# A hybrid HGRN2/Hyena inference step on one core: the prompt's spectrum and the gating on GpSimd, one w_out tile between the inverse transforms, and two products by halves

## The chip, the cores and the metric

The kernel runs on one core of one Trainium2 chip. The metric is the device time of a whole execution in microseconds (us), median over the runs shown. Inside the core five engines run their own instruction streams and meet only at semaphores: TensorE (PE), VectorE (DVE), ScalarE (ACT), GpSimd (POOL) and SyncE (SP), the last of which only issues DMAs. PE writes its results to eight PSUM banks, DVE and ACT empty them.

## What is computed

One layer of a diffusion backbone for two groups of tokens, a prompt of 128 and a sample of 512, held together as 640 columns (five tiles of 128). Weights and activations are fp32. Cut to what matters here:

```
proj = h @ w_in                      # q, forget gates, values, gate, and hy (v, x1, x2)
o_hg = HGRN2 scan of both directions, normed, * silu(g)       # 512 channels
u    = x1 * v
z    = long_conv(u, kern) + hy_d * u # by FFT: transform, * spectrum of kern, transform back
y_hy = x2 * z * rsqrt(mean((x2 * z)**2) + eps) * hy_norm_w    # 512 channels
x    = x + g1 * (concat(o_hg, y_hy) @ w_out)
x    = x + g2 * convffn(rmsnorm(x) * (1 + sc2) + sh2)
```

## The kernel before, in words

Every engine's program is written out by hand, in order, inside one function `build`, with semaphore waits between them; nothing is scheduled by a planner. An fp32 product is made of three products of rounded halves (`w_hi`, `w_lo` and `h_hi`, `h_lo`): `split_product` issues them, `split_hi` (ACT) and `split_lo` (DVE) make the two halves of a weight unit of 128 x 1024, in four slots used in turn. `link` makes an engine wait for its own last instruction.

The stretch that the change touches lies between the HGRN2 heads and the second norm, from 386 to 475 us of the profiled execution. It does this:

- The product with `w_out` is cut into two halves of its input channels. The first half (`o_hg`) is made first: ten output tiles of 128 tokens x 512 columns (five token tiles times two column halves `n`), in PSUM banks 6 and 7 in turn. Each is copied by ACT into `x1` (`raw_taken`), multiplied with the gate row `grow1` on DVE (`gate_raw`), and a DMA of GpSimd's queue with an adding write then puts the residual `x` on top (`ld_res`).
- Meanwhile DVE multiplies the sample's spectrum `U` with the filter's (`multiply(0)`, `multiply(1)`, ten instructions each, the second of which raises `zspec_ready` to 2) and the prompt's spectrum `Up` with its own filter (seven instructions, `zspec_ready` 3).
- The inverse transforms follow on PE, one pair for each block `c` of 128 channels: `z_sample(c)` (8 matmuls, 16 records in the trace, for each of four blocks) and `z_prompt(c)`, in two pairs of banks. ACT takes them out (`zc`, which gives `z_taken` and `z_ready`), DVE makes `x2 * z` (`yhy_ready`) and splits it into `h_hi`, `h_lo` (`split_y`, `y_split`), ACT squares it into the one buffer `sq` (`ysq_ready`), and PE sums the squares over the channels with a column of ones (`sum_channels(c)`, `ysq_used`).
- `mix(i)` is the second half of the product with `w_out` for token tile `i`: both column halves, four channel blocks each. `mix_tile(i)` on DVE scales it, gates it, and adds it to `x1`; norm, transposes (`turn_tile`) and the first FFN products (`half_product`) follow.

Of the kernel before, what the change touches and what calls it, by code (L numbers as in the profile page):

```python
# [385 lines left out]
def build(nc, io):  # L386
# [12 lines left out]
    with ctx:  # L399
# [407 lines left out]
        def _(eng):  # L807
# [72 lines left out]
            eng.wait_ge(sem("zspec_ready"), 3)  # L880
# [10 lines left out]
        def _(eng):  # L891
# [60 lines left out]
            eng.wait_ge(sem("silu_in"), 1)  # L952
            A(gate_c, gate_c, ACT.Exp).then_inc(sem("silu_exp"), 1)
# [6 lines left out]
            eng.wait_ge(sem("bound_in"), 1)  # L960
            A(bound[:, 1, :], bound[:, 0, :], ACT.Exp).then_inc(sem("bound_exp"), 1)
# [155 lines left out]
            for n in range(2):  # L1117
                for i in range(NT):
                    eng.wait_ge(sem("hg_mixed"), n * NT + i + 1)
                    A(x1[:, n, i, :], ps[:, HG_BANKS[(n * NT + i) % 2], :], ACT.Copy).then_inc(sem("raw_taken"), 1)  # L1120
                for k in range(2):
                    split_hi(UNIT_WOUT + 4 + 2 * n + k)


# [238 lines left out]
        def _(eng):  # L1363
# [145 lines left out]
            eng.wait_ge(sem("bound_exp"), 1)  # L1509
# [188 lines left out]
            eng.wait_ge(sem("up_ready"), 1)  # L1698
            r, t = prod[:, 0, 0, :], prod[:, 1, 0, :]
            link(V.tensor_tensor(r, Up[:, 0, :], kspec_p[:, 0, :], ALU.mult))  # L1700
            link(V.tensor_tensor(t, Up[:, 1, :], kspec_p[:, 1, :], ALU.mult))
            link(V.tensor_tensor(r, r, t, ALU.subtract))
            link(V.tensor_tensor(t, Up[:, 0, :], kspec_p[:, 1, :], ALU.mult))
            link(V.tensor_tensor(Up[:, 1, :], Up[:, 1, :], kspec_p[:, 0, :], ALU.mult))
            link(V.tensor_tensor(Up[:, 1, :], Up[:, 1, :], t, ALU.add))
# [989 lines left out]
```

## Time and profile before

| | |
|---|---|
| median of 3 runs | 913.55 us (912.89 to 916.66) |
| the profiled execution | 912.88 us, of which the span of the trace is 911.1 us |
| PE busy | 887.6 us, 97% of the span |
| DVE busy | 717.0 us, 79% |
| ACT busy | 443.3 us, 49% |
| GpSimd busy | 38.9 us, 4%, 58 instructions |
| granted TensorE clock, mean | 0.996 of full speed |

The busy times of different engines overlap and can't be added. PE is busy for nearly all of the span, so what counts is where PE waits, and for whom. The times of day in the rows below are microseconds from the start of the span.

### The profile page before, as it was taken

How to read it: one execution, taken by the hardware profiler on the slowest of the kernel's cores; microseconds unless marked ns; L12 is line 12 of the kernel's file. 1: busy time of each engine (PE TensorE's matmuls, PEld its weight loads, DVE VectorE, ACT ScalarE, POOL GpSimd, SP SyncE). 2: the span in 40 equal slices, each digit the busy share in tenths (PEclk: the TensorE clock that was granted, in tenths of full speed). 3: DMA queues.
4: the chain of work that ended last, by engine and by line, in shares of the span. 5: the costliest groups of instructions: out<-in, count | busy, mean ns of one | idle time of the engine just before them, and what ended most of it. 6: DMA issues, size and time to landing. Idle time of an engine off the chain costs nothing.

```text
span 911.1 us, 14075 instructions
## 1 busy us (share of the span) xinstructions
PE 887.6 (97%) x5374; PEld 788.7 (87%) x5374; DVE 717.0 (79%) x911; ACT 443.3 (49%) x710; POOL 38.9 (4%) x58
## 2 busy tenths in 40 slices
PE   7999999999999999999899999999999999999997
PEld 4479898898898898688779999999999999998885
DVE  5744755966966985699678899999999999988645
ACT  5745324334343323332276756556565656565443
POOL 2200000100000000002000000000000000000000
PEclk9999999999999999999999999999999999999999
DMA  8765233144134244325511232233313232345703
GB/s 297 244 217 174 83 126 138 37 157 145 63 122 145 91 164 137 89 70 112 144 46 48 76 131 99 97 110 114 115 62 130 108 111 88 131 152 202 261 0 116
DMA packets 39275, 112.76 MB, mean 124 GB/s; under 512 B 4471, under 2 KB 12663, under 8 KB 38568
## 3 DMA queue, kind: packets, MB, share of 16 engines
q1 hardware_dynamic: 33944, 93.58, 30.3%
q0 software_dynamic: 4800, 17.99, 6.5%
q8 instruction: 43, 0.70, 0.3%
q10 hardware_dynamic: 464, 0.30, 0.1%
q14 instruction: 24, 0.20, 0.1%
HBM read 101.48 MB, written 10.37 MB: 123 GB/s over the span
## 4 chain that ended last, share of the span: by engine, by line
PE 84%; DVE 9%; ACT 3%; issue 2%; DMA 1%; ACTq 0%; DVEq 0%; POOLq 0%
PE ps L2005 19%; PE ps L2006 19%; PE ps L2007 19%; PE ps L2505 14%; PE ps L2226 4%; PE ps L2025 2%; PE ps L2086 2%; PE ps L2238 1%; PE ps L2363 1%; DMA part<-in_rates 1%; DVE w_lo L1377 1%; PE ps L2033 1%; PE ps L2246 1%; DMA w<-in_hy_w 1%; ACT xn L1154 1%
## 5 line engine op out<-in xcount | busy, mean ns | idle before, releaser
L2005 PE MATMUL ps<-h_hi,w_hi 128*128 128x320 f32 x620 | 196.3, 317 | 2.8 <-DVE w_lo L1377 1.4
L2007 PE MATMUL ps<-h_hi,w_lo 128*128 128x320 f32 x620 | 191.6, 309 | 0.0
L2006 PE MATMUL ps<-h_lo,w_hi 128*128 128x320 f32 x620 | 191.5, 309 | 0.0
L2005 PEld LDWEIGHTS ps<-h_hi,w_hi 128*128 128x128 f32 x620 | 116.6, 188 | 4.1 <-issue 3.1
L2006 PEld LDWEIGHTS ps<-h_lo,w_hi 128*128 128x128 f32 x620 | 116.6, 188 | 0.0
L2007 PEld LDWEIGHTS ps<-h_hi,w_lo 128*128 128x128 f32 x620 | 116.4, 188 | 0.0
L1868 DVE TENSOR_TENSOR w_lo<-raw,w_hi 128x1024 fp32r<-128x1024 f32 (+1 forms) x53 | 64.2, 1212 | 18.6 <-ACT w_hi L1220 17.6
L1220 ACT ACTIVATE w_hi<-raw 128x1024 fp32r<-128x1024 f32 (+1 forms) x53 | 55.5, 1047 | 31.8 <-PE ps L2007 31.7
L1377 DVE TENSOR_TENSOR w_lo<-raw,w_hi 128x1024 fp32r<-128x1024 f32 x44 | 53.4, 1224 | 6.4 <-ACT w_hi L904 5.2
L2005 PE MATMUL ps<-w_hi,h_hi 128*128 128x512 f32 x120 | 49.6, 413 | 2.0 <-DVE h_lo L1734 2.0
L904 ACT ACTIVATE w_hi<-raw 128x1024 fp32r<-128x1024 f32 x44 | 45.8, 1057 | 4.4 <-DMA raw<-in_slots 2.4
L2007 PE MATMUL ps<-w_hi,h_lo 128*128 128x512 f32 x120 | 47.4, 395 | 0.0
L2006 PE MATMUL ps<-w_lo,h_hi 128*128 128x512 f32 x120 | 47.3, 394 | 0.0
L1868 DVE TENSOR_TENSOR w_lo<-wsum,w_hi 128x1024 fp32r<-128x1024 f32 x38 | 46.4, 1221 | 1.0 <-ACT w_hi L1220 0.4
L2505 PE MATMUL ps<-t_hi,w_hi 128*128 128x320 f32 x152 | 47.0, 309 | 0.1
L2005 PE MATMUL ps<-t_hi,w_hi 128*128 128x320 f32 x152 | 47.0, 309 | 0.0
L2006 PE MATMUL ps<-t_lo,w_hi 128*128 128x320 f32 x152 | 47.0, 309 | 0.0
L2007 PE MATMUL ps<-t_hi,w_lo 128*128 128x320 f32 x152 | 47.0, 309 | 0.0
L2505 PE MATMUL ps<-h_hi,w_lo 128*128 128x320 f32 x152 | 47.0, 309 | 0.0
L2505 PE MATMUL ps<-t_hi,w_lo 128*128 128x320 f32 x152 | 47.0, 309 | 0.0
L2505 PE MATMUL ps<-t_lo,w_hi 128*128 128x320 f32 x152 | 47.0, 309 | 0.0
L2505 PE MATMUL ps<-h_lo,w_hi 128*128 128x320 f32 x152 | 46.9, 309 | 0.0
(320 smaller groups left out, 2067.2 us busy)
## 6 DMA issues: line engine op xcount, KB each, us to landing
raw<-in_slots SPq DMA_DIRECT2D x138, 512.0 KB, 4.7
acts<-actf POOLq DMA_DIRECT2D x22, 320.0 KB, 2.5
raw<-in_slots SPq DMA_DIRECT2D x24, 256.0 KB, 6.5
xf<-acts SPq DMA_DIRECT2D x12, 320.0 KB, 6.6
wsum<-acts SPq DMA_DIRECT2D x10, 320.0 KB, 7.7
xin<-in_x_sample SPq DMA_DIRECT2D x4, 512.0 KB, 11.2
grow<-gates POOLq DMA_DIRECT2D x2, 1024.0 KB, 12.3
x<-in_x_sample POOLq DMA_DIRECT2D x2, 1024.0 KB, 13.7
```

The lines of the kernel that those rows point to most:

```text
L904: A(w_hi[:, n % SPLITS, :], src, ACT.Copy).then_inc(sem("hi_ready"), 1)
L1154: A(xn[:, i % 2, :].rearrange("p (n c) -> p n c", c=HW), x1[:, :, i, :], ACT.Copy, scale=stat[:, 1, 1, i:i + 1]).then_inc(sem("xn_ready"), 1)
L1220: A(split_target(w_hi, t, slot), src, ACT.Copy).then_inc(sem("hi_ready"), 1)
L1377: V.tensor_tensor(w_lo[:, n % SPLITS, :], raw[:, r % RING, :], w_hi[:, n % SPLITS, :].bitcast(F32), ALU.subtract).then_inc(sem("lo_ready"), 1)
L1868: link(V.tensor_tensor(split_target(w_lo, t, slot), src, split_target(w_hi, t, slot).bitcast(F32), ALU.subtract), "lo_ready")
L2005: mm(out, lhs[0], rhs[0], start=first, stop=False)
L2006: mm(out, lhs[0], rhs[1], start=False, stop=False)
L2007: return mm(out, lhs[1], rhs[0], start=False, stop=last)
L2025: last = mm(ps[g * GROUP:(g + 1) * GROUP, bank, :], silu_c[:, GROUPS * j + g, :], piece[:, g % 2 * HW:(g % 2 + 1) * HW], start=(j == 0), s ...
L2086: last = mm(ps[:, 4 + 2 * cs + e, :], ktab[:, cs, e, k, m * P:(m + 1) * P], filt[:, cs, 2 * e + k, :], start=(k == 0), stop=(k == 1))
L2226: last = mm(chunk(h, j, c), kc[:, l % 2, c * P:(c + 1) * P], ap(QQ, c * P, [(2 * s, P // (2 * s)), (T + s, 2), (1, s)]), start=True, stop= ...
L2505: done = mm(ps[:, bank, 0:HT], w[i], r[j], start=False, stop=(k == NC - 1 and i == 1), skip_group_check=True)
```

## The change

Four things are done at once. The seven instructions on the prompt's spectrum go from DVE to GpSimd (semaphore `up_multiplied`). The gating of the ten raw tiles goes from DVE (two instructions for each column half, over 2048 and 512 columns) to GpSimd (one instruction of 512 columns for each tile, as soon as ACT has copied that tile). The tenth tile of the first half product (`raw_tile(1, NT - 1)`) goes behind `z_prompt(1)`, and each `z_prompt(c)` stands right behind its `z_sample(c)`. And `mix(0)` and `mix(1)` are made by column halves: first `n = 0` of both, then `n = 1` of both; with it the weight units 6 and 7 are split later, `split_hi` inside ACT's loop over `c` (after the squares of blocks 1 and 2), and `split_lo` behind DVE's loop. Some semaphores of the early stages are merged under new names (`filter_dma`, `exp_done`, `filter_made`); those waits stay what they were.

```diff
--- before.py
+++ after.py
+            link = linker(eng, "pool_own")
...
-            load(ktab[:, :, :, :, :], io["ktab"], "ld_ktab")
-            load(ptab_k[:, :, :], io["ptab"][:, 0], "ld_ktab")
+            load(ktab[:, :, :, :, :], io["ktab"], "filter_dma")
+            load(ptab_k[:, :, :], io["ptab"][:, 0], "filter_dma")
...
+            eng.wait_ge(sem("up_ready"), 1)
+            r, t = sq[:, 0:HW], x1[:, 1, NT - 1, :]
+            G = nc.gpsimd.tensor_tensor
+            link(G(r, Up[:, 0, :], kspec_p[:, 0, :], ALU.mult))
+            link(G(t, Up[:, 1, :], kspec_p[:, 1, :], ALU.mult))
+            link(G(r, r, t, ALU.subtract))
+            link(G(t, Up[:, 0, :], kspec_p[:, 1, :], ALU.mult))
+            link(G(Up[:, 1, :], Up[:, 1, :], kspec_p[:, 0, :], ALU.mult))
+            link(G(Up[:, 1, :], Up[:, 1, :], t, ALU.add))
+            link(nc.gpsimd.tensor_copy(Up[:, 0, :], r), "up_multiplied")
+            eng.wait_ge(sem("ld_gate1"), 16)
             for n in range(2):
                 cols = slice(n * HW, (n + 1) * HW)
-                eng.wait_ge(sem("raw_gated"), n + 1)
+                for i in range(NT):
+                    eng.wait_ge(sem("raw_taken"), n * NT + i + 1)
+                    x = x1[:, n, i, :]
+                    nc.gpsimd.tensor_tensor(x, x, grow1[:, int(i == NT - 1), cols], ALU.mult).then_inc(sem("raw_gated"), 1)
+                eng.wait_ge(sem("raw_gated"), (n + 1) * NT)
                 eng.dma_start(x1[:, n, 0:NT - 1, :], io["x_sample"][0].rearrange("(i p) c -> p i c", p=P)[:, :, cols],
                               accum_op=ALU.add).then_inc(sem("ld_res"), 16)
                 eng.dma_start(x1[:, n, NT - 1, :], io["x_prompt"][0][:, cols], accum_op=ALU.add).then_inc(sem("ld_res"), 16)
-            eng.wait_ge(sem("zspec_ready"), 3)
+            eng.wait_ge(sem("zspec_ready"), 2)
             load(grow2[:, :, :], gates[1].partition_broadcast(P), "ld_gate2")
...
+            def take_raw(n, i):
+                eng.wait_ge(sem("hg_mixed"), n * NT + i + 1)
+                if n * NT + i == 2 * NT - 1:
+                    eng.wait_ge(sem("up_multiplied"), 1)
+                A(x1[:, n, i, :], ps[:, HG_BANKS[(n * NT + i) % 2], :], ACT.Copy).then_inc(sem("raw_taken"), 1)
             eng.wait_ge(sem("udft"), 5)
             A(Up[:, :, :], banks(UDFT_PROMPT, 2 * 512), ACT.Copy).then_inc(sem("up_ready"), 1)
             for n in range(2):
-                for i in range(NT):
-                    eng.wait_ge(sem("hg_mixed"), n * NT + i + 1)
-                    A(x1[:, n, i, :], ps[:, HG_BANKS[(n * NT + i) % 2], :], ACT.Copy).then_inc(sem("raw_taken"), 1)
-                for k in range(2):
-                    split_hi(UNIT_WOUT + 4 + 2 * n + k)
+                for i in range(NT - n):
+                    take_raw(n, i)
+                if n == 0:
+                    for k in range(2):
+                        split_hi(UNIT_WOUT + 4 + k)
...
+                if c == 1:
+                    take_raw(1, NT - 1)
                 eng.wait_ge(sem("yhy_ready"), c + 1)
                 if c:
                     eng.wait_ge(sem("ysq_used"), c)
                 A(sq[:, 0:TS].rearrange("p (r c) -> p r c", c=GRID), grid(x2, c * CONV), ACT.Square)
                 A(sq[:, TS:T], x2[:, c, PADS:CONV], ACT.Square).then_inc(sem("ysq_ready"), 1)
+                if 0 < c < NC - 1:
+                    split_hi(UNIT_WOUT + 5 + c)
...
-            eng.wait_ge(sem("up_ready"), 1)
-            r, t = prod[:, 0, 0, :], prod[:, 1, 0, :]
-            link(V.tensor_tensor(r, Up[:, 0, :], kspec_p[:, 0, :], ALU.mult))
-            link(V.tensor_tensor(t, Up[:, 1, :], kspec_p[:, 1, :], ALU.mult))
-            link(V.tensor_tensor(r, r, t, ALU.subtract))
-            link(V.tensor_tensor(t, Up[:, 0, :], kspec_p[:, 1, :], ALU.mult))
-            link(V.tensor_tensor(Up[:, 1, :], Up[:, 1, :], kspec_p[:, 0, :], ALU.mult))
-            link(V.tensor_tensor(Up[:, 1, :], Up[:, 1, :], t, ALU.add))
-            link(V.tensor_copy(Up[:, 0, :], r), "zspec_ready")
-            def gate_raw(n):
-                eng.wait_ge(sem("raw_taken"), (n + 1) * NT)
-                x = x1[:, n, 0:NT - 1, :]
-                link(V.tensor_tensor(x, x, ap(grow1, n * HW, [(0, NT - 1), (1, HW)]), ALU.mult))
-                x = x1[:, n, NT - 1, :]
-                link(V.tensor_tensor(x, x, ap(grow1, D + n * HW, [(1, HW)]), ALU.mult), "raw_gated")
-            eng.wait_ge(sem("ld_gate1"), 16)
-            gate_raw(0)
             for k in range(2):
                 split_lo(UNIT_WOUT + 4 + k)
-            gate_raw(1)
...
-                if c < 2:
-                    split_lo(UNIT_WOUT + 6 + c)
+            for k in range(2):
+                split_lo(UNIT_WOUT + 6 + k)
...
-            for n in range(2):
+            def raw_tile(n, i):
                 units = [unit_ready(UNIT_WOUT + 2 * n + p) for p in range(2)]
...
+                at = n * NT + i
+                if at == 0:
+                    eng.wait_ge(sem("uspec_ready"), 2)
+                if at >= 2:
+                    eng.wait_ge(sem("raw_taken"), at - 1)
+                for k in range(NC):
+                    last = split_product(ps[:, HG_BANKS[at % 2], :], [x[:, k, i * P:(i + 1) * P] for x in (h_hi, h_lo)],
+                                         [w[:, k % 2 * HW:(k % 2 + 1) * HW] for w in units[k // 2]], k == 0, k == NC - 1)
+                last.then_inc(sem("hg_mixed"), 1)
+            for at in range(2 * NT - 1):
+                raw_tile(*divmod(at, NT))
...
-                    eng.wait_ge(sem("zspec_ready"), 3)
+                    eng.wait_ge(sem("up_multiplied"), 1)
...
             z_sample(0)
+            z_prompt(0)
             z_sample(1)
-            z_prompt(0)
+            z_prompt(1)
+            raw_tile(1, NT - 1)
             z_sample(2)
-            z_prompt(1)
+            z_prompt(2)
             z_sample(3)
+            z_prompt(3)
             eng.wait_ge(sem("raw_taken"), 2 * NT)
             sum_channels(0)
-            z_prompt(2)
             sum_channels(1)
-            z_prompt(3)
-            units = [unit_ready(UNIT_WOUT + 4 + p) for p in range(4)]
             def mix(i, ns=(0, 1)):
-                order = [(n, k) for n in ns for k in range(NC, KD)]
-                if i == 0:
-                    order.sort(key=lambda step: step[1])
-                for n, k in order:
+                units = {n: [unit_ready(UNIT_WOUT + 4 + 2 * n + p) for p in range(2)] for n in ns}
+                for n, k in [(n, k) for n in ns for k in range(NC, KD)]:
                     if i == 0 and n == 0:
                         if k == KD - 1:
                             sum_channels(2)
                         eng.wait_ge(sem("y_split"), k - NC + 1)
                     last = split_product(ps[:, MIX_BANKS[i] + n, :], [x[:, k, i * P:(i + 1) * P] for x in (h_hi, h_lo)],
-                                         [w[:, k % 2 * HW:(k % 2 + 1) * HW] for w in units[2 * n + (k - NC) // 2]],
+                                         [w[:, k % 2 * HW:(k % 2 + 1) * HW] for w in units[n][(k - NC) // 2]],
                                          k == NC, k == KD - 1)
                     if i == NT - 1 and k == KD - 1:
                         last.then_inc(sem("wout_used"), 1)
                     elif k == KD - 1 and n == 1:
                         last.then_inc(sem("mixed"), 1)
-                if i == 0:
-                    sum_channels(3)
             def turn_tile(i):
                     if k % 4 == 3:
                         last.then_inc(sem("x_turned"), 1)
-            mix(0)
-            mix(1)
+            mix(0, (0,))
+            sum_channels(3)
+            mix(1, (0,))
+            mix(0, (1,))
+            mix(1, (1,))
             mix(2)
             turn_tile(0)
             mix(3, (0,))
```

PE's queue, at the inverse transforms, before. `ps<-tab,U` is `z_sample`, `ps<-ptab,Up` is `z_prompt`, `ps<-ones,sq` is `sum_channels`, and the rows with `w_hi`, `w_lo` are first the last raw tile and then `mix(0)`.

```order
L2007 MATMUL ps<-w_hi,h_lo 128x512
L2404 MATMUL ps<-tab,U 128x256 x16
L2415 MATMUL ps<-ptab,Up 128x128 x2
L2404 MATMUL ps<-tab,U 128x256 x8
L2415 MATMUL ps<-ptab,Up 128x128 x2
L2404 MATMUL ps<-tab,U 128x256 x8
L2390 MATMUL ps<-ones,sq 128x1 x5
L2415 MATMUL ps<-ptab,Up 128x128 x2
L2390 MATMUL ps<-ones,sq 128x1 x5
L2415 MATMUL ps<-ptab,Up 128x128 x2
L2005 MATMUL ps<-w_hi,h_hi 128x512
```

The same place of the changed kernel. The first row is the end of the ninth raw tile, and the three rows between the second and the third transform are the start of the tenth.

```order
L2017 MATMUL ps<-w_hi,h_lo 128x512
L2418 MATMUL ps<-tab,U 128x256 x8
L2429 MATMUL ps<-ptab,Up 128x128 x2
L2418 MATMUL ps<-tab,U 128x256 x8
L2429 MATMUL ps<-ptab,Up 128x128 x2
L2015 MATMUL ps<-w_hi,h_hi 128x512
L2016 MATMUL ps<-w_lo,h_hi 128x512
L2017 MATMUL ps<-w_hi,h_lo 128x512
...
L2418 MATMUL ps<-tab,U 128x256 x8
L2429 MATMUL ps<-ptab,Up 128x128 x2
L2418 MATMUL ps<-tab,U 128x256 x8
L2429 MATMUL ps<-ptab,Up 128x128 x2
L2404 MATMUL ps<-ones,sq 128x1 x10
L2015 MATMUL ps<-w_hi,h_hi 128x512
```

Twelve matmuls of a raw tile moved in between the transforms, and both first sums of squares now stand behind all four transforms.

GpSimd's queue before, from the load of the inverse table on. The rows are DMAs only, the second to fifth the adding ones.

```order
L809 DMA tab<-in_itab 128x2048 [waits udft]
L877 DMA x<-in_x_sample 128x4x512 [waits raw_gated]
L879 DMA x<-in_x_prompt 128x512
L877 DMA x<-in_x_sample 128x4x512 [waits raw_gated]
L879 DMA x<-in_x_prompt 128x512
```

And in the changed kernel, where the tile `sq` and the last tile of `x1` serve as its work space:

```order
L809 DMA tab<-in_itab 128x2048 [waits udft]
L879 TENSOR_TENSOR sq<-Up,kspec_p 128x512 [waits up_ready]
L880 TENSOR_TENSOR x<-Up,kspec_p 128x512 [waits pool_own]
L881 TENSOR_TENSOR sq<-sq,x 128x512 [waits pool_own]
L882 TENSOR_TENSOR x<-Up,kspec_p 128x512 [waits pool_own]
L883 TENSOR_TENSOR Up<-Up,kspec_p 128x512 [waits pool_own]
L884 TENSOR_TENSOR Up<-Up,x 128x512 [waits pool_own]
L885 COPY Up<-sq 128x512 [waits pool_own]
L893 TENSOR_TENSOR x<-x,grow 128x512 [waits raw_taken,ld_gate1,up_multiplied]
L893 TENSOR_TENSOR x<-x,grow 128x512 [waits raw_taken] x4
L895 DMA x<-in_x_sample 128x4x512 [waits raw_gated]
L897 DMA x<-in_x_prompt 128x512
```

Seventeen computing instructions are new on GpSimd, all but the copy with two SBUF inputs; five more `x<-x,grow` and two more DMAs follow the last row.

ACT's queue in the loop over the channel blocks, changed kernel, from the eviction of block 1 to that of block 2. Before, the same rows stood there without the row `x<-ps` and without the row `w_hi<-raw`.

```order
L1154 ACTIVATE zc<-ps,knorm 128x2x256 [waits yhy_ready,z_made]
L1158 ACTIVATE zc<-ps,knorm 128x128 [waits zp_made]
L1136 ACTIVATE x<-ps 128x512 [waits up_multiplied,hg_mixed]
L1165 ACTIVATE sq<-x 128x512 [waits ysq_used,yhy_ready]
L1166 ACTIVATE sq<-x 128x128
L922 ACTIVATE w_hi<-raw 128x1024 [waits hg_mixed,raw_in2]
L1154 ACTIVATE zc<-ps,knorm 128x2x256 [waits yhy_ready,z_made]
```

The copy of the tenth raw tile and the rounding of weight unit 6 came in ahead of the eviction of block 2.

## Rows read from the trace of the kernel before

**Rows 1.** The page's span and the chain that ended last, by engine.

```profile
span 911.1 us, 14075 instructions
...
PE 84%; DVE 9%; ACT 3%; issue 2%; DMA 1%; ACTq 0%; DVEq 0%; POOLq 0%
```

**Rows 2.** PE's waits, 387 to 474 us: line waited for, us, times, longest.

```profile
PE ps L2005 <- DVE h_lo L1734: 2.0, 2, 1.5
PE ps L2005 <- DVE w_lo L1377: 1.4, 1, 1.4
PE ps L2404 <- ACT zc L1129: 1.1, 1, 1.1
PE ps L2390 <- ACT sq L1139: 0.4, 1, 0.4
```

**Rows 3.** Timeline of PE: start, us, instruction, [idle before <-releaser].

```profile
387.65 0.80 PE L2005 MATMUL ps<-w_hi,h_hi 128*128 128x512 f32 x1
...
415.31 7.07 PE L2404 MATMUL ps<-tab,U 128*128 128x256 f32 x32
422.22 0.61 PE L2415 MATMUL ps<-ptab,Up 128*128 128x128 f32 x4
...
431.37 1.17 PE L2390 MATMUL ps<-ones,sq 128*128 128x1 f32 x10
...
435.10 0.47 PE L2005 MATMUL ps<-w_hi,h_hi 128*128 128x512 f32 x1
...
457.86 1.03 PE L2460 MATMUL ps<-ident,xn 128*128 128x128 f32 x8
```

**Rows 4.** Timeline of DVE in the same stretch.

```profile
389.11 1.22 DVE L1377 TENSOR_TENSOR w_lo<-raw,w_hi 128x1024 fp32r<-128x1024 f32 x1
390.25 1.22 DVE L1677 TENSOR_TENSOR prod<-U,kspec 128x1024 f32<-128x1024 f32 x1
...
410.44 0.69 DVE L1688 TENSOR_TENSOR U<-U,prod 128x512 f32<-128x512 f32 x1
411.16 0.69 DVE L1700 TENSOR_TENSOR prod<-Up,kspec_p 128x512 f32<-128x512 f32 x1
...
424.35 0.88 DVE L1739 SCALAR_TENSOR_TENSOR zc<-u_hy,vec,zc 128x640 f32<-128x640 f32 x1
...
428.34 1.22 DVE L1377 TENSOR_TENSOR w_lo<-raw,w_hi 128x1024 fp32r<-128x1024 f32 x1
```

**Rows 5.** Timeline of ACT in the same stretch.

```profile
388.25 1.03 ACT L1114 ACTIVATE Up<-ps 128x1024 f32<-128x1024 f32 x1 [1.12 <-PE ps L2369]
...
402.40 2.00 ACT L904 ACTIVATE w_hi<-raw 128x1024 fp32r<-128x1024 f32 x2
...
432.64 0.63 ACT L1138 ACTIVATE sq<-x 128x512 f32<-128x512 f32 x1 [4.64 <-PE ps L2390]
```

**Rows 6.** Timeline of GpSimd, 21 to 45 us and 424 us.

```profile
21.70 1.26 POOL L838 TENSOR_TENSOR filt<-filt 1x512 f32<-1x512 f32 x1 [1.87 <-DVE filt L1465]
...
38.49 1.28 POOL L849 TENSOR_TENSOR feats<-feats,decay 128x512 f32<-128x512 f32 x1 [14.83 <-DVE decay L1473]
41.84 1.79 POOL L849 TENSOR_TENSOR feats<-feats,decay 128x512 f32<-128x512 f32 x1 [2.07 <-DVE decay L1473]
...
425.37 1.52 POOL L879 DMA_DIRECT2D x<-in_x_prompt  x1
```

**Rows 7.** Timeline of DVE beside those GpSimd instructions.

```profile
22.29 0.70 DVE L1444 TENSOR_TENSOR mod<-mod,vec 128x8 f32<-128x8 f32 x1
...
41.80 0.69 DVE L1473 TENSOR_TENSOR size<-size 128x512 f32<-128x512 f32 x1
42.52 0.69 DVE L1491 TENSOR_TENSOR kspec<-ps,part 128x512 f32<-128x512 f32 x1
```

**Rows 8.** That DVE line over the whole trace: shortest/median/longest ns.

```profile
L1444 DVE TENSOR_TENSOR mod<-mod,vec x12: 166/166/699, 22.3 to 363.1; 128x8 f32<-128x8 f32 x12
```

**Rows 9.** Windows: us, busy of PE, PEld, DVE, ACT, POOL, granted clock, DMA.

```profile
438.00:442.00 4.00, 2.78 (x17) 2.32 (x16) 3.61 (x8) 0.88 (x4) 0.00 (x0) 1.00 1.09 332
442.00:446.00 4.00, 3.26 (x10) 2.70 (x11) 0.65 (x2) 0.20 (x2) 0.00 (x0) 0.61 0.36 150
```

More of the change, by code:

```diff
@@ L951, in _ @@
             eng.wait_ge(sem("ld_vec"), 16)
-            eng.wait_ge(sem("silu_in"), 1)
-            A(gate_c, gate_c, ACT.Exp).then_inc(sem("silu_exp"), 1)
+            eng.wait_ge(sem("exp_in"), 1)
+            A(gate_c, gate_c, ACT.Exp).then_inc(sem("exp_done"), 1)
             eng.wait_ge(sem("ld_rates"), 16)
@@ L959, in _ @@
                   bias=rates[:, bias:bias + 1]).then_inc(sem("decay_ready"), 1)
-            eng.wait_ge(sem("bound_in"), 1)
-            A(bound[:, 1, :], bound[:, 0, :], ACT.Exp).then_inc(sem("bound_exp"), 1)
+            eng.wait_ge(sem("exp_in"), 2)
+            A(bound[:, 1, :], bound[:, 0, :], ACT.Exp).then_inc(sem("exp_done"), 1)
             A(stat[:, 2, 0, 0:1], eps[:, :], ACT.Sqrt)
@@ L1427, in _ @@
             eng.wait_ge(sem("ld_vec"), 16)
-            link(V.tensor_scalar(gate_c, v("c", 0, 2 * KD), -1.0, 80.0, ALU.mult, ALU.min), "silu_in")
+            link(V.tensor_scalar(gate_c, v("c", 0, 2 * KD), -1.0, 80.0, ALU.mult, ALU.min), "exp_in")
             lb = v("lb_f", 0, 2 * NC)
-            link(V.tensor_tensor(bound[:, 0, :], lb, lb, ALU.subtract), "bound_in")
+            link(V.tensor_tensor(bound[:, 0, :], lb, lb, ALU.subtract), "exp_in")
             def sum_groups(e):
@@ L1508, in _ @@
             join(0)
[L1509 removed]
+            eng.wait_ge(sem("exp_done"), 2)
             link(V.reciprocal(bound[:, 2, :], bound[:, 1, :]))
@@ L1749, in _ @@
             link(V.reciprocal(rhy[:, 2, :], rhy[:, 1, :]))
+            eng.wait_ge(sem("ld_gate1"), 16)
             def mix_tile(i):
@@ L2049, in tap_pair @@
                         if d:
-                            last.then_inc(sem("taps_made"), 1)
+                            last.then_inc(sem("filter_made"), 1)
             def tap_prompt():
@@ L2058, in tap_prompt @@
                     last = mm(ps[:, d, :], hid[halves[d], 1, at:at + P], w3sd[halves[d], d, :], start=True, stop=True)
-                last.then_inc(sem("taps_made"), 1)
+                last.then_inc(sem("filter_made"), 1)
             def tap_sums():
@@ L2109, in _ @@
             mm(ps[0:NHID, 0, 0:SIDE], w1[0:NEMB, :], feats[0:NEMB, 0:SIDE], start=True, stop=True)
-            mm(ps[NHID:P, 0, 0:SIDE], w1[0:NEMB, :], feats[0:NEMB, SIDE:2 * SIDE], start=True, stop=True).then_inc(sem("hid_made"), 1)
+            mm(ps[NHID:P, 0, 0:SIDE], w1[0:NEMB, :], feats[0:NEMB, SIDE:2 * SIDE], start=True, stop=True).then_inc(sem("filter_made"), 1)
             keep_busy(4)
@@ L2115, in _ @@
                 last = mm(ps[rows, 0, 0:SIDE], w2[rows, :], hid[rows, 0, :], start=True, stop=True)
-            last.then_inc(sem("hid_made"), 1)
+            last.then_inc(sem("filter_made"), 1)
             keep_busy(4)
@@ L2128, in _ @@
             ada_turn(0)
-            eng.wait_ge(sem("ld_ktab"), 32)
+            eng.wait_ge(sem("filter_dma"), 32)
             filter_dft(0)
@@ L2366, in _ @@
             eng.wait_ge(sem("uspec_ready"), 1)
-            eng.wait_ge(sem("ld_ptab"), 16)
+            eng.wait_ge(sem("spectra_dma"), 16)
             for cs in range(2):
@@ L2373, in _ @@
             eng.wait_ge(sem("heads_split"), 1)
-            for n in range(2):
+            def raw_tile(n, i):
                 units = [unit_ready(UNIT_WOUT + 2 * n + p) for p in range(2)]
-                for i in range(NT):
-                    at = n * NT + i
-                    if at == 0:
-                        eng.wait_ge(sem("uspec_ready"), 2)
-                    if at >= 2:
-                        eng.wait_ge(sem("raw_taken"), at - 1)
-                    for k in range(NC):
-                        last = split_product(ps[:, HG_BANKS[at % 2], :], [x[:, k, i * P:(i + 1) * P] for x in (h_hi, h_lo)],
-                                             [w[:, k % 2 * HW:(k % 2 + 1) * HW] for w in units[k // 2]], k == 0, k == NC - 1)
-                    last.then_inc(sem("hg_mixed"), 1)
+                at = n * NT + i
[9 more added lines that the diff above has]
+                raw_tile(*divmod(at, NT))
             def sum_channels(c):
```

11 lines of the change are left out of this document (5 added, 6 removed).

## The prediction

> **What bounds the kernel now.** I read the page first. The chain that ended last is PE's for 84% [rows 1], so the time changes only where PE waits, gets more to do, or runs at a lower clock. Next I asked for PE's waits in the touched stretch [rows 2]. They are few: 2.0 us for DVE's split of `y`, 1.1 us for ACT's eviction of a transform, 0.4 us for squares, and later 1.4 us for a weight split. Then I laid PE's timeline [rows 3] beside DVE's and ACT's [rows 4, 5]. From 387.65 to 415.31 PE makes ten raw tiles without a pause, 27.66 / 10 = 2.8 us each. The transforms start at 415.31, the second product (`mix`) at 435.10, and the first transposes, behind `mix(2)`, at 457.86. So the stretch from the first transform to the end of `mix(2)` takes 42.6 us now. It includes 1.1 + 0.4 + 2.0 = 3.5 us of waits, and a lower clock: the window 442 to 446 was granted 0.61 [rows 9], between the levels 1.2 and 2.4 GHz, after PE had been busy for 2.78 of the 4 us before it. With 3.26 us of busy time at 0.61, about 3.26 x 0.39 = 1.3 us were lost to it.
>
> DVE is the second queue to watch. From 390.25 to 411.13 it multiplies the sample's spectrum (20 instructions, first and last in [rows 4]), and the first transform can't start before that. It is 4.2 us ahead of PE there (411.13 against 415.31), and that margin is what the change works on from both sides.
>
> **What the change takes away.** DVE loses the seven instructions of the prompt's spectrum and the four of the gating, which with the two weight splits fill it from 411.16 to 424.35 [rows 4]. With 2 x 1.2 us of splits left, that is 10.8 us less work on DVE. None of it was waited for by PE except through the eviction wait of 1.1 us. PE loses no work. With the tenth raw tile moved, its ninth ends at 415.31 - 2.8 = 412.5, so the first transform could start 2.8 us earlier, and those 2.8 us are spent again after `z_prompt(1)`.
>
> **What it adds on GpSimd, and to whom.** The new work is six TENSOR_TENSORs and a copy from 389.3 on, when `Up` is there [rows 5], then five gatings, two DMA issues, five gatings, two DMA issues. One TENSOR_TENSOR of 128x512 takes 1.28 us there when DVE is idle [rows 6]. GpSimd alone would need 6 x 1.3 + 0.6 = 8.4 us for the spectrum, done by 398, long before PE asks for it.
>
> But the two engines get in each other's way. DVE's `mod<-mod,vec`, with two SBUF inputs, takes 166 ns in the median of 12 and 699 ns once [rows 8]. That once is at 22.29, while GpSimd's TENSOR_TENSOR ran from 21.70 to 22.96. DVE's ended at 22.99, just behind it [rows 6, 7]. The other way round, GpSimd's instruction at 41.84 took 1.79 instead of 1.28 us. DVE had begun one with two SBUF inputs at 41.80 and ended it at 42.49. From there to 43.63, GpSimd's end, are 1.14 us. DVE's next, with one input in PSUM (42.52), was not slowed [rows 7]. I read this as: a DVE instruction with two SBUF inputs and a computing instruction of GpSimd wait for each other's end. All 20 multiplications of `U` have both inputs in SBUF.
>
> The page "SBUF — State Buffer" of the Trainium skill ("Who interferes with whom") says this as a rule: a VectorE instruction with two SBUF inputs contends with a GpSimd instruction that reads SBUF, and whichever issues first holds the shared ports for its whole length. The rows show it once in each direction, the one with DVE as the loser only against an instruction of one partition and for 0.53 us. By the rule each GpSimd instruction costs DVE its whole length, which is the forecast below; by the 0.53 us alone it would be the second rival.
>
> The price: each engine has one instruction waiting while the other runs, so they take turns. GpSimd's gap to its next is about 0.1 us, shorter than any DVE instruction here (0.69 or 1.22), so after each DVE instruction GpSimd's turn comes. Going by turns, GpSimd has its spectrum after seven turns, at about 390.3 + 6 x 1.14 + 0.5 + 6 x 1.25 = 405, and goes straight on to tiles 0 to 4, whose copies are done. It then issues DMAs for about 2.2 us and gates tiles 5 to 8, all before DVE has done its 20. That is 15 TENSOR_TENSORs x 1.14 + 0.5 for the copy = 17.6, minus some 0.3 us of gaps, 17.3 us in DVE's way: 411.1 + 17.3 = 428.4 instead of 411.1. The first transform starts at 428.4, 13.1 us later than before. PE's ninth tile ended at 412.5, so PE idles 16 us.
>
> **From there to the end of `mix(2)`.** A transform is 7.07 / 2 = 3.5 us, `z_prompt` about 0.45, a sum 1.15, a quarter of a mix tile 0.69. PE: blocks 0 and 1 and the raw tile until 439.0, blocks 2 and 3 until 446.9, `sum_channels(0)` until 448.0. That last is the catch in the order: ACT's squares of block 1 need it (`ysq_used`) because `sq` is one buffer, and ACT evicts block 2 only behind them. Before it was no different (the squares at 432.64 waited 4.64 us for PE's sum [rows 5]), but now the rounding of unit 6 (1.0 us, half of the row at 402.40) stands there too. So: squares until 448.9, rounding until 449.9, eviction until 450.9, DVE's block 2 (424.35 to 428.34, 4.0 us [rows 4]) until 455.0. PE has two quarters to do meanwhile, since the `n = 1` quarters no longer stand between: it waits 1.0 us for the squares and 3.5 us for `y_split` 3. Block 3 goes the same way: squares at 453.0, rounding of unit 7, eviction until 455.9, DVE until 460.0, a PE wait of 3.1 us. Then the last quarter, `sum_channels(3)` and 20 quarters: 460.0 + 0.7 + 1.15 + 13.8 = 475.6. That is 47.2 us from the first transform against 42.6: plus 2.8 for the tile, plus 7.6 instead of 3.5 of waits, minus the clock's 1.3 and roundings.
>
> The clock: PE starts the transforms after 16 us of idleness and waits over 3 us twice in `mix`. Before, 1.5 us idle after a half-idle stretch was enough for a window at 0.61. I expect three such windows at 1.3 each; bounds 1.3 and 5. I take 3.
>
> Behind `mix(2)` everything shifts alike: `mix_tile(1)` then ends about 3 us before PE is through, as now, and the DMAs with the residual (issued by about 442, up to 15 us) are in before `mix_tile(0)` at 466.
>
> **Sum.** 13.1 + 4.6 + 3 = 20.7 us later on an execution of 912.9 us (span 911.1, and 1.8 around it): 933.6. The runs' median is 0.6 above the profiled one, so I say **933.5**.
>
> **Rivals.**
> *DVE wins each turn.* Its next instruction follows 0.03 us after the last, and GpSimd may not get in between; no row shows who wins. Then `U` is ready at 411, GpSimd's spectrum only starts there and, among DVE's splits, ends near 422, and `z_prompt(0)`, due at 416.0, waits 6 us. From then on as above (4.6), with 2.8 us gained at the start: 912.9 - 2.8 + 6 + 4.6 + 2 clock = 922.7.
> *Each costs DVE 0.53 us, what the row shows, no more.* 15 x 0.53 + 0.2 = 8 us: transforms from 419.2, 3.9 us late, 912.9 + 3.9 + 4.6 + 3 = 924.4.
> *No contention at 128 partitions.* Transforms from 412.5: -2.8 + 4.6 + 2 at most = 3.8, so 916.7, within 0.5% or just over it.
> *Faster.* No contention, and DVE's freed 10.8 us carry through, so that block 2 is evicted without the wait. All 3.5 us of waits and the low clock's 1.3 vanish: 908.1. It decides whether ACT gets `ysq_used` 1 before the third transform is done. The order of PE's queue puts the sum behind the fourth, so I give it little.
> *The spectrum on GpSimd doesn't matter, only the order does.* That is the case without contention, above.
>
> **How the numbers follow.** Chances: turns 0.58, DVE first or the partial price 0.22 together, no contention 0.15, faster 0.05. A bound for the turns: with 1.28 for 1.14 DVE ends 2.1 us later, and with 5 us of clock the sum is 937.7. With 1.0 and 1.3 us of clock it is about 929.5. That is the likeliest case's own range, 929 to 938. The range for 8 in 10 reaches down over the two middle cases and most of the no-contention case: 917 to 939. About 0.5% (4.6 us) can be told from no change: no contention lies half within, which gives faster 0.05, same 0.10, slower 0.85.
>
> **What would show it.** Right: PE idle for some 16 us before the first transform, released by DVE's last `U`; DVE's 0.69 and 1.22 us rows at 1.8 and 2.4 between 390 and 428; GpSimd's at about 2.4; two PE waits of some 3 us at `mix(0, (0,))`; a window of half clock at the first transform. Wrong: DVE's multiplications at their old durations, `zspec_ready` at 411, or a long wait at `z_prompt(0)` for GpSimd. If DVE keeps its pace, the prediction is wrong by the 13 us of that one step and by most of the clock's 3.

## The result, and the profile after

The changed kernel takes 939.0 us (median of 4 runs, 938.79 to 939.55), the kernel before 914.25 in the same comparison (4 runs). The ratio is 1.0269, 95% interval 1.0245 to 1.0292: slower by about 25 us. The profiled execution has a span of 937.0 us, 25.9 more than before.

PE's waits in the touched stretch of the changed kernel, 387 to 505 us (line waited for, us, times, longest); it answers to [rows 2].

```profile
PE ps L2418 <- issue: 15.9, 1, 15.9
PE ps L2015 <- DVE h_lo L1742: 4.1, 2, 3.0
PE ps L2015 <- DVE w_lo L1406: 1.4, 1, 1.4
PE ps L2404 <- ACT sq L1166: 1.0, 1, 1.0
```

One wait of 15.9 us is new, at the first inverse transform. The view names no engine for it ("issue"). The timeline of DVE tells who it was; these are its multiplications of `U`, with a few rows left out, and answer to [rows 4]:

```profile
391.71 2.33 DVE L1706 TENSOR_TENSOR prod<-U,kspec 128x1024 f32<-128x1024 f32 x1
394.07 2.20 DVE L1707 TENSOR_TENSOR prod<-U,kspec 128x1024 f32<-128x1024 f32 x1
...
405.26 0.98 DVE L1713 TENSOR_TENSOR U<-prod,U 128x512 f32<-128x512 f32 x1
406.29 1.67 DVE L1714 TENSOR_TENSOR U<-prod,U 128x512 f32<-128x512 f32 x1
...
415.84 7.47 DVE L1708 TENSOR_TENSOR prod<-prod 128x1024 f32<-128x1024 f32 x1
423.35 1.22 DVE L1709 TENSOR_TENSOR prod<-U,kspec 128x1024 f32<-128x1024 f32 x1
...
429.31 0.69 DVE L1717 TENSOR_TENSOR U<-U,prod 128x512 f32<-128x512 f32 x1
```

And GpSimd's timeline beside them (answers to [rows 6]):

```profile
390.82 2.13 POOL L879 TENSOR_TENSOR sq<-Up,kspec_p 128x512 f32<-128x512 f32 x1 [2.01 <-ACT Up L1139]
393.04 2.16 POOL L880 TENSOR_TENSOR x<-Up,kspec_p 128x512 f32<-128x512 f32 x1
...
404.21 1.49 POOL L885 COPY Up<-sq 128x512 f32<-128x512 f32 x1
405.79 8.94 POOL L893 TENSOR_TENSOR x<-x,grow 128x512 f32<-128x512 f32 x5
415.03 1.32 POOL L895 DMA_DIRECT2D x<-in_x_sample  x1 [0.31 <-POOL x L893]
415.86 1.43 POOL L897 DMA_DIRECT2D x<-in_x_prompt  x1
416.43 5.79 POOL L893 TENSOR_TENSOR x<-x,grow 128x512 f32<-128x512 f32 x4
```

While GpSimd computes, a DVE instruction of 1.22 us takes 2.20 and one of 0.69 takes 1.67; GpSimd's of 1.28 take 2.16. One DVE instruction, at 415.84, takes 7.47 us: it ends about when the four gatings behind GpSimd's two DMA issues are done. From 423.35 on GpSimd is idle and DVE's are at 1.22 and 0.69 again. The twenty end at 430.00, 38.3 us after the first began, against 20.9 before.

PE's timeline (answers to [rows 3]):

```profile
430.10 6.23 PE L2418 MATMUL ps<-tab,U 128*128 128x256 f32 x16 [15.89 <-issue]
436.16 0.61 PE L2429 MATMUL ps<-ptab,Up 128*128 128x128 f32 x4
436.61 3.62 PE L2418 MATMUL ps<-tab,U 128*128 128x256 f32 x16
...
459.07 0.79 PE L2015 MATMUL ps<-w_hi,h_hi 128*128 128x512 f32 x1 [2.99 <-DVE h_lo L1742]
460.52 2.13 PE L2404 MATMUL ps<-ones,sq 128*128 128x1 f32 x10
...
483.53 1.03 PE L2468 MATMUL ps<-ident,xn 128*128 128x128 f32 x8
```

And the windows in which its clock was low (us, busy of PE, PEld, DVE, ACT, POOL, granted clock, DMA; answers to [rows 9]):

```profile
430.00:434.00 4.00, 3.90 (x9) 3.16 (x10) 2.36 (x2) 0.00 (x0) 0.00 (x0) 0.50 0.40 122
456.00:460.00 4.00, 1.01 (x3) 0.83 (x3) 3.09 (x7) 2.62 (x5) 0.00 (x0) 0.50 0.27 115
460.00:464.00 4.00, 2.88 (x13) 2.60 (x12) 3.75 (x8) 0.83 (x2) 0.00 (x0) 0.50 0.01 2
464.00:468.00 4.00, 4.00 (x15) 3.62 (x16) 2.30 (x4) 0.30 (x1) 0.00 (x0) 0.50 0.43 147
468.00:472.00 4.00, 4.00 (x10) 3.07 (x10) 0.18 (x1) 0.00 (x0) 0.00 (x0) 0.50 0.34 119
472.00:476.00 4.00, 4.00 (x17) 3.28 (x16) 0.00 (x0) 0.00 (x0) 0.00 (x0) 0.90 0.00 0
```

The 25.9 us come in three pieces. Everything ahead of the stretch is 1.4 us later; 1.0 of it is there at 30 us already, in code that the change only renames. In the profiled executions of the ten variants below, which share that code, the raw tiles start 0.6 to 2.5 us later than before, so I leave this piece out of the account. The first transform moved from 415.31 to 430.10: 14.8, of which 13.4 belong to the change. From there to the first transposes behind `mix(2)` it is 53.4 us instead of 42.6, 10.9 more with rounding: 2.8 for the moved tile, 5.1 instead of 3.5 us of waits, and a remainder of 6.5, which I put down to the clock. The rows bear that out: the first transform alone takes 6.23 instead of 3.62 us, and behind 459 ten matmuls of a sum of squares take 2.13 instead of some 1.17.

### The profile page after: what moved, and what is told of

Its sections match the earlier page's. It is cut to its first block, busy times and chain, and to the rows that moved or that the text cites. A ratio compares the mean times of both kernels' runs of the same rounds, so it can differ in the third digit from the quotient of the medians.

```text
span 937.0 us, 14114 instructions
## 1 busy us (share of the span) xinstructions
PE 895.4 (96%) x5374; PEld 794.1 (85%) x5374; DVE 725.3 (77%) x900; ACT 443.0 (47%) x710; POOL 68.4 (7%) x75
## 4 chain that ended last, share of the span: by engine, by line
PE 83%; DVE 7%; ACT 4%; issue 4%; DMA 2%; ACTq 0%; DVEq 0%; SPq 0%; POOLq 0%
PE ps L2015 18%; PE ps L2016 18%; PE ps L2017 18%; PE ps L2516 14%; PE ps L2236 3%; PE ps L2035 2%; PE ps L2418 2%; PE ps L2096 1%; PE ps L2373 1%; PE ps L2248 1%; DMA part<-in_rates 1%; PE ps L2043 1%; PE ps L2256 1%; DVE tmix L1770 1%; DMA w<-in_hy_w 1%
## 5 line engine op out<-in xcount | busy, mean ns | idle before, releaser
L1406 DVE TENSOR_TENSOR w_lo<-raw,w_hi 128x1024 fp32r<-128x1024 f32 x44 | 53.4, 1224 | 6.5 <-ACT w_hi L922 5.4
L2016 PE MATMUL ps<-w_lo,h_hi 128*128 128x512 f32 x120 | 48.2, 402 | 0.0
```

What stands on the lines that cost most here:

```text
L1406: V.tensor_tensor(w_lo[:, n % SPLITS, :], raw[:, r % RING, :], w_hi[:, n % SPLITS, :].bitcast(F32), ALU.subtract).then_inc(sem("lo_ready"), 1)
L2016: mm(out, lhs[0], rhs[1], start=False, stop=False)
```

## The experiments

All times are compared with the kernel before on the same chip and in the same rounds; ratios are those of that comparison.

**e1_order: GpSimd's arithmetic back on DVE.** PE's and ACT's new order stays.

```diff
-            link(G(r, Up[:, 0, :], kspec_p[:, 0, :], ALU.mult))    # and six more, on GpSimd
-                    nc.gpsimd.tensor_tensor(x, x, grow1[...], ALU.mult)
+            link(V.tensor_tensor(r, Up[:, 0, :], kspec_p[:, 0, :], ALU.mult))   # and six more
+            gate_raw(0)                    # behind them, on DVE
+                if c == 1:
+                    gate_raw(1)            # in DVE's loop, behind split_y(1)
```

> The changed kernel with all GpSimd arithmetic back on DVE (the seven spectrum instructions behind the multiplications of U, the gating as two instructions for each column half, the second half behind block 1), and the new order of PE and ACT kept. If contention between DVE and GpSimd is the cause, DVE's twenty multiplications take 20.9 us again, the first transform starts about 12 us earlier than in the changed kernel, and only the order's price stays: 917 to 922 us. If the order is what costs (late squares, late eviction of block 2), it stays near 935 to 939.

918.92 us, ratio 1.0053 (1.0031 to 1.0076). DVE's multiplications are at 1.22 and 0.69, the first transform starts at 414.43. So 20 of the 25 us are the arithmetic on GpSimd, and 4 to 5 the order. PE's waits for `y` and for squares are 4.8 and 1.0 us here, against 3.5 of all kinds in the same stretch before, and the windows from 442 to 450 were granted 0.50: the order's price is made of both.

```profile
414.43 3.62 PE L2423 MATMUL ps<-tab,U 128*128 128x256 f32 x16
```

```profile
PE ps L2020 <- DVE h_lo L1745: 4.8, 2, 3.1
```

**e2_pool: the complement.** GpSimd's work stays, the order of PE, of ACT and of the weight splits is the old one.

```diff
-            for at in range(2 * NT - 1):
+            for at in range(2 * NT):                 # ten raw tiles first
-            mix(0, (0,)); sum_channels(3); mix(1, (0,)); mix(0, (1,)); mix(1, (1,))
+            mix(0); sum_channels(3); mix(1)          # mix(0) by channel blocks
```

> The complement: GpSimd's spectrum and gating kept, and the order of PE, ACT and of the weight splits as before the change (ten raw tiles first, mix(0) by channel blocks). If contention is the cause, DVE's last multiplication ends near 431, the first transform starts some 15 us later than before the change, one cold stretch of PE is added, and the time is 928 to 935 us. If the order is the cause, 914 to 918 us.

931.69 us, ratio 1.0199 (1.0172 to 1.0225). PE waits 14.4 us at the first transform, which starts at 430.91. Five gatings follow GpSimd's first DMA issues here, and the DVE instruction beside them takes 8.69 us:

```profile
415.43 8.69 DVE L1703 TENSOR_TENSOR prod<-prod 128x1024 f32<-128x1024 f32 x1
```

The two complements add up to more or less the whole: 0.53% + 1.99% against 2.69%.

**e3_spectrum: only the spectrum on GpSimd**, the gating on DVE as in e1_order.

```diff
-                    nc.gpsimd.tensor_tensor(x, x, grow1[...], ALU.mult)
+            gate_raw(0)        # on DVE, as in e1_order
```

> The changed kernel with only the seven spectrum instructions on GpSimd, the gating back on DVE. The price by turns is about 1.0 to 1.1 us for each GpSimd instruction: DVE's multiplications end near 418 to 419 (27 to 28 us instead of 37), the time is 922 to 926 us. If GpSimd's DMA issues or the gating instructions alone did the damage, the multiplications stay at 21 us and the time is that of the order alone, 917 to 922 us.

926.93 us, ratio 1.0139 (1.0108 to 1.0171). DVE's timeline, from the sixth multiplication on:

```profile
403.30 2.20 DVE L1706 TENSOR_TENSOR U<-U,prod 128x1024 f32<-128x1024 f32 x1
405.53 0.98 DVE L1708 TENSOR_TENSOR U<-prod,U 128x512 f32<-128x512 f32 x1
406.55 0.69 DVE L1709 TENSOR_TENSOR U<-prod,U 128x512 f32<-128x512 f32 x1
```

The first six are long, the seventh by 0.29 (beside GpSimd's copy), and at once, with GpSimd's seven done, all is as before. The twenty take 391.98 to 419.15, 27.2 us. That is 6.3 us for six instructions and a copy, 1.0 us each.

**e4_late: GpSimd starts behind DVE's last multiplication.**

```diff
+            eng.wait_ge(sem("zspec_ready"), 2)
             eng.wait_ge(sem("up_ready"), 1)
```

> The changed kernel, with GpSimd waiting for DVE's last multiplication before it starts. The same arithmetic then contends with cheaper work of DVE. Contention: the multiplications take 20.9 us, the first transform starts at 412 to 414, z_prompt(0) waits for GpSimd until about 421, and the time is 922 to 930 us. If instead the spectrum merely moved to a slower engine were the cause, the late start would make it worse than the changed kernel, above 939 us.

928.8 us, ratio 1.0164 (1.0137 to 1.0191): 10 us better than the changed kernel with one more wait. The multiplications take 20.9 us, and PE now waits for GpSimd itself at `z_prompt(0)`, the wait that one of the rivals had foreseen, 5.6 us:

```profile
PE ps L2430 <- POOL Up L886: 5.6, 1, 5.6
```

It is still 1.6% slower than the kernel before. In DVE's timeline stands a row of 7.47 us for an instruction of 0.35. It is the last of a `split_y`, beside five gatings behind two DMA issues:

```profile
429.73 1.38 DVE L1739 TENSOR_SCALAR h_hi<-x,vec 128x512 fp32r<-128x512 f32 x1
...
432.26 7.47 DVE L1743 SCALAR_TENSOR_TENSOR h_lo<-x,vec,h_hi 128x128 fp32r<-128x128 f32 x1
```

**e5_chained: each gating waits for the one before.**

```diff
-  nc.gpsimd.tensor_tensor(x, x, grow1[...], ALU.mult).then_inc(sem("raw_gated"), 1)
+  link(nc.gpsimd.tensor_tensor(x, x, grow1[...], ALU.mult), "raw_gated")
```

> The changed kernel, with each of GpSimd's ten gating instructions waiting for the one before it. In the changed kernel a batch of four without such waits, right behind two DMA issues, kept one DVE instruction waiting for all of it (7.47 us for one of 1.22), where the chained ones let DVE in after each. If the batch holds the ports because its instructions overlap, no DVE row between 391 and 432 is longer than 2.5 us here, and the time is 1 to 3 us below the changed kernel's (936 to 938). If DVE's loss is only GpSimd's total time, the long row is replaced by several of 2.2 us and the time stays at 938 to 940.

936.47 us, ratio 1.0253 (1.0227 to 1.0278). The one row of 7.47 us is gone, and turns are taken again:

```profile
416.21 2.85 DVE L1709 TENSOR_TENSOR prod<-U,kspec 128x1024 f32<-128x1024 f32 x1
419.09 2.17 DVE L1710 TENSOR_TENSOR U<-U,kspec 128x1024 f32<-128x1024 f32 x1
421.29 2.17 DVE L1711 TENSOR_TENSOR U<-U,prod 128x1024 f32<-128x1024 f32 x1
423.49 1.63 DVE L1713 TENSOR_TENSOR U<-prod,U 128x512 f32<-128x512 f32 x1
```

The four gatings cost DVE 1.63 + 0.95 + 0.95 + 0.94 = 4.5 us here and 7.47 - 1.22 = 6.25 in the changed kernel. The trace shows the 1.8 us (the twenty take 36.5 us instead of 38.3). The 2.5 us between the medians fit, but the intervals of the two ratios overlap, so the time alone doesn't show it. One row, 2.85, is longer than I had said.

**e6_writes: memsets in the place of GpSimd's arithmetic.** It leaves out the prompt's product with its filter and the gating.

```diff
-            link(G(r, Up[:, 0, :], kspec_p[:, 0, :], ALU.mult))
+            link(nc.gpsimd.memset(r, 0.0))          # seven such, and ten on x
```

> The changed kernel with each of GpSimd's seventeen new instructions replaced by a memset to zero of the same 128x512 tile, with the same waits. It leaves out the product of the prompt's spectrum with its filter and the gating of the raw tiles. It tells what of GpSimd's instruction DVE waits for. If DVE waits for GpSimd's reads of SBUF, its twenty multiplications take 20.9 us again and the time is that of the order alone, 917 to 921 us. If any computing instruction on GpSimd holds DVE up, writes too, DVE's rows are longer by the length of the memsets beside them and the first transform comes past 418, 922 us or more.

919.91 us, ratio 1.0047 (1.0032 to 1.0062), that of e1_order. GpSimd's memset and DVE's multiplication at the same time, from the two timelines:

```profile
391.59 0.53 POOL L879 MEMSET sq<- 128x512 f32 x1
392.18 0.53 POOL L879 MEMSET x<- 128x512 f32 x1
```

```profile
391.33 1.22 DVE L1700 TENSOR_TENSOR prod<-U,kspec 128x1024 f32<-128x1024 f32 x1
392.59 1.23 DVE L1701 TENSOR_TENSOR prod<-U,kspec 128x1024 f32<-128x1024 f32 x1
```

Neither is lengthened. GpSimd's being busy, its semaphores and its writes don't disturb DVE. The memsets are also shorter (0.53 us), but twelve of them lie beside DVE's twenty multiplications, and not one of those is longer. What the memsets lack is reads of SBUF and arithmetic. GpSimd's COPY, which reads one tile and computes nothing, did cost DVE 0.29 us (e3_spectrum), so it is the reads that the runs point to; none of them takes away the arithmetic alone. The Trainium skill's page "SBUF — State Buffer" ("Who interferes with whom") says that a DVE instruction with two SBUF inputs does not contend with a GpSimd instruction that only writes SBUF, and the trace agrees.

**e8_tile and e9_halves: the order in its two parts**, all arithmetic on DVE. e8_tile is e1_order with

```diff
+                    order.sort(key=lambda step: step[1])   # mix(0) by channel blocks again
+                        split_hi(UNIT_WOUT + 6 + k)        # both, right behind take_raw(1, 4)
+                        split_lo(UNIT_WOUT + 6 + k)        # both, behind split_y(1)
```

and e9_halves is the order of before but for

```diff
-            mix(0); mix(1)
+            mix(0, (0,)); sum_channels(3); mix(1, (0,)); mix(0, (1,)); mix(1, (1,))
-                if c < 2:
-                    split_lo(UNIT_WOUT + 6 + c)
+            for k in range(2):                     # behind the loop
+                split_lo(UNIT_WOUT + 6 + k)
```

> Everything on DVE as in e1_order, and the halves of mix(0) and mix(1) undone (channel blocks first, both column halves together; weight units 6 and 7 split right behind the moved tile and in the middle of DVE's loop). Only the moved tile and the order of the transforms are left of the change. By the walk through the queues DVE's last split of y comes at the same time as before: 912 to 916 us, no difference that can be told. If the moved tile is what costs the 4 us of e1_order, 917 to 920.

912.72 us, ratio 1.0000 (0.9986 to 1.0015).

> Everything on DVE, ten raw tiles first and the transforms in the old order; only mix(0) and mix(1) are made by column halves, with the splits of units 6 and 7 behind DVE's loop. PE has half as much to do between two blocks of y: its waits at mix(0) grow from 2.0 to about 4 us and the clock falls to half there. 915 to 919 us. If the halves are harmless and the 4 us of e1_order belong to the tile, 912 to 915.

917.53 us, ratio 1.0046 (1.0031 to 1.0061). So the moved tile costs and gains nothing, and the order's price is that of the halves. But not as I had said: PE's waits for `y` don't grow to 4 us.

```profile
PE ps L2014 <- DVE h_lo L1741: 1.3, 2, 0.9
```

What grew is the time at half clock. Windows of e9_halves:

```profile
434.00:438.00 4.00, 3.58 (x22) 3.03 (x20) 2.42 (x5) 1.93 (x6) 0.00 (x0) 0.83 1.12 206
438.00:442.00 4.00, 3.11 (x11) 2.25 (x10) 3.75 (x8) 1.11 (x4) 0.00 (x0) 0.50 1.01 332
442.00:446.00 4.00, 3.58 (x14) 3.20 (x15) 3.69 (x5) 0.83 (x2) 0.00 (x0) 0.50 0.08 20
446.00:450.00 4.00, 4.00 (x12) 3.34 (x13) 0.37 (x2) 0.30 (x1) 0.00 (x0) 0.50 0.68 244
```

Before, one window was granted 0.61 [rows 9]; here it is half clock (1.2 GHz) from about 437 to 450. At half clock the same few quarters last longer, and so fill the wait that they would have left. What stands behind them pays. It is not this one execution: the mean granted clock is 0.989 to 0.994 in the eight runs of e9_halves, and 0.992 to 0.997 in the 25 of the kernel before beside them.

Why the clock fell there is open. The halves alone don't explain it: it fell at about 436.8, within the first quarter of `mix(0)`, up to which PE's queue is the same in both kernels, and PE had been as busy before it as in the kernel before, where the clock stayed. The two windows are of the kernel before and of e9_halves:

```profile
433.00:437.00 4.00, 3.57 (x23) 3.17 (x23) 3.83 (x7) 1.75 (x5) 0.00 (x0) 1.00 1.09 268
```

```profile
433.00:437.00 4.00, 3.58 (x27) 3.29 (x27) 1.85 (x3) 1.68 (x4) 0.00 (x0) 0.96 1.13 207
```

**e10_fill and e11_first: can the stretch be made faster?** All arithmetic on DVE, raw tiles first, and the products still by halves. The waits for the blocks of `y` are filled with quarters of `mix(1)` and `mix(2)`. The edit is shown in short; `quarter(i, k)` is channel block `k` of `mix(i, (0,))`.

```diff
+            z_sample(0); z_prompt(0); ... z_sample(2); z_prompt(2)
+            sum_channels(0)                  # ahead of z_sample(3)
+            quarter(0, 4); quarter(0, 5)
+            quarter(2, 4); quarter(2, 5)     # waits z_taken 3, for its bank
+            quarter(0, 6); quarter(2, 6); sum_channels(2)
+            quarter(1, 4); quarter(1, 5); quarter(1, 6)
+            quarter(0, 7); sum_channels(3); quarter(1, 7); quarter(2, 7)
+            mix(0, (1,)); mix(1, (1,)); mix(2, (1,))
```

The splits `split_lo` 6 and 7 stand behind DVE's loop, and `gate_raw(1)` behind `split_y(0)`.

> A version meant to beat both, everything on DVE: the waits of PE for the blocks of y are filled with quarters of mix(1) and mix(2) (n = 0, as soon as their banks are free), sum_channels(0) stands ahead of the fourth transform so that ACT is not held, and the weight splits 6 and 7 stand behind DVE's loop. DVE's last split of y then comes about 2 us earlier, PE has no wait above 1 us there, and no window at half clock: 908 to 911 us. If PE's waits in this stretch are not what bounds it, 913 to 916.

911.25 us, ratio 0.9971 (0.9959 to 0.9983): faster than before, if by less than 0.5%, and just above the 908 to 911 that I expected. PE waits 0.4 us for `y` and the windows from 430 to 458 are all at 1.00. What was won there is partly given back behind it: PE waits 1.4 us at `turn_tile(0)`, where it waited for nothing before, since the norm has to follow `mix_tile(0)`, for which DVE sat idle 3.5 us.

```profile
448.48 1.29 DVE L1770 SCALAR_TENSOR_TENSOR tmix<-ps,rhy,grow 128x1024 f32<-128x1024 f32 x1 [3.50 <-PE ps L2017]
```

e11_first puts `mix(0, (1,))` ahead of `quarter(1, 7)` and `quarter(2, 7)`:

```diff
+            quarter(0, 7); sum_channels(3); mix(0, (1,))
+            quarter(1, 7); mix(1, (1,)); quarter(2, 7); mix(2, (1,))
```

> e10_fill with the n = 1 half of mix(0) ahead of the last quarters (k = 7, n = 0) of tiles 1 and 2, so that mix_tile(0), for which DVE sat idle 3.5 us, starts 1.4 us earlier, and with it the norm and the first transposes, for which PE waited 1.4 us. 909 to 911 us, up to 1.4 below e10_fill (911.2). If that chain is not what bounds the stretch now, the same as e10_fill.

910.67 us, ratio 0.9952 (0.9935 to 0.9969). The wait at `turn_tile(0)` fell from 1.4 to 0.7 us and DVE's from 3.5 to 2.2. The two were compared with the kernel before at different times, and their ratios' intervals overlap: that e11_first is better than e10_fill is not shown. Both beat the kernel before.

## Why the prediction was right

Forecast 933.5, range 917 to 939, measured 939.0. The side and the mechanism were right. The size was so in part by luck: 939.0 lies above the 929 to 938 that the prediction gave for its own case of turns, and at the very end of the wide range. Part of the 5.5 us is a slip: the sum's 933.6 is for a profiled execution, and with the 0.6 by which the median lies above it, the forecast should have read 934.2. In profiled executions 20.7 us were forecast and 25.9 measured.

- **DVE and GpSimd take turns.** Forecast 17.3 us more for DVE's twenty, measured 17.4 (38.3 - 20.9). e1_order and e3_spectrum show it causally. That the sum came out is luck. The 1.14 us each, read from one row of [rows 6] and its neighbour in [rows 7], measured 1.0 by turns, less than GpSimd's own 1.27. The last four gatings cost 6.25 instead of 4.6: they did not take turns at all, and the prediction had no such case.
- **The first transform later by 13.1 us**: 13.4.
- **The rival "0.53 us only"** and the rival without contention fell: no row shows less than 0.94 for a TENSOR_TENSOR by turns. **"DVE wins each turn"** did not happen. e4_late makes its schedule by hand, and gives 928.8; I had worked out 922.7 for it. GpSimd's gating holds up DVE's blocks of `y` there, but PE's waits for `y` and squares are 5.6 us, no more than the 5.8 of e1_order, where nothing contends. What is more is mostly the clock: the second transform, behind the 5.6 us at `z_prompt(0)`, takes 6.00 instead of 3.62 us, and the windows from 452 to 460 were granted 0.50.

```profile
424.57 6.00 PE L2419 MATMUL ps<-tab,U 128*128 128x256 f32 x16
```

- **From the transform to the end of `mix(2)`.** Waits of 7.6 us were forecast, 1.0 for the squares and 3.5 and 3.1 for `y`. Measured are 1.0, 3.0 and 1.1. The walk through ACT's queue held in its order: the eviction of block 2 came behind the squares and the rounding. DVE was through with block 2 at 459.0 and with block 3 at 463.7, forecast for 455.0 and 460.0. Of these some 4 us, 1.7 were there when the first transform started, and the rest is that transform's half clock, which the walk didn't have in it. The walk also lost 1.0 us: 42.6 + 2.8 + 4.1 - 1.3 is 48.2, not 47.2, and the difference was called roundings.
- **The clock: the term that was too small.** "I expect three such windows at 1.3 each; bounds 1.3 and 5. I take 3." Against the 42.6 us of before with its 1.3, that is 3 us. Measured is 2.6 in the first transform, and half clock without a break from the wait at 456 until about 472. The two forecast waits shrank for it (by 2.5 us together), since PE itself was slower between them. Waits and clock together were forecast at 7.6 + 3 and measured at 5.1 + 7.8, where 7.8 is the remainder of 6.5 above and the 1.3 of before. That is 2.3 more. Another 1.4 came ahead of the stretch, 1.0 is the walk's, and 0.3 the first transform's: 5.0 of the 5.2 us.
- **The order.** I charged 4.6 us and some clock to it. e1_order measures 4 to 5 in all. It belongs to the halves (e9_halves), none of it to the moved tile alone (e8_tile). I had read it as waits. Of that, e1_order shows 2.3 us (5.8 instead of 3.5), e9_halves none; there it is all half clock, the fall of which no run explains.

## What to carry to other kernels

Elementwise work moved to GpSimd is not free beside DVE instructions that read two SBUF operands: each GpSimd TENSOR_TENSOR cost DVE 1.0 us here, of its own 1.27. It was free beside a DVE instruction with one input in PSUM [rows 7], but not beside every one with a single SBUF tensor (below). Look for a single row of either engine that is too long, and price the move by it. If DVE's output is waited for, leave the work on DVE; to start GpSimd only when DVE has delivered gave 10 us back with one wait (e4_late), and was still slower than no move. And where PE waits in small pieces, try to fill them with independent matmuls: e10_fill has the halves of e9_halves and the filling, and no window at half clock from 430 to 458. That the same work spread thinner brings the clock down by itself is not shown.

## What the runs showed of the hardware that I had not expected

- GpSimd instructions without a wait between them, right behind two DMA issues, let DVE in only when all are done: 7.47 us for one DVE instruction of 1.22 (four of them), 8.69 for one of 1.22 (five, e2_pool), and 7.47 for one of 0.35 (five, e4_late). The rows of the four are 2.12 to 2.15 us long at starts 1.2 apart, so they overlap one another. Chained, they take turns (e5_chained). The five without chains ahead of the DMA issues took turns as well (DVE at 1.67). That the overlap comes from the DMA issues is my inference; no run took those away.
- DVE's TENSOR_SCALAR with a single SBUF tensor was held up too, 1.38 instead of 0.49 us (e4_late). GpSimd's COPY, with one input, was lengthened from 0.61 to 1.49, and itself cost DVE 0.29. A GpSimd memset cost DVE nothing, and took 0.53 us but for one of 0.91 right behind two DMA issues.
- Half clock stayed for some 16 us in the changed kernel, the last 8 of them with PE busy all the time (windows 464 to 472). In the kernel before it was over some 4 us after PE's last wait (at 442.74), in e9_halves after some 7 (at 443.45).
